# TensorE's expert loop starts on a fetch block boundary and announces its closing branch

## The reference

```python
logits = (t @ w_router + b_router).astype(jnp.float32)
top_val, top_idx = lax.top_k(logits, TOP_K)          # 4 of 32
gate_w = jax.nn.softmax(top_val, axis=-1)
...
def expert_block(args):
    tok_idx, e = args
    xb = t_pad[tok_idx]
    hb = xb @ w_exp_in[e] + b_exp_in[e]               # 1024 -> 2 x 1024
    g = jnp.minimum(hb[:, :D_FF_2], SWIGLU_LIMIT)
    u = jnp.clip(hb[:, D_FF_2:], -SWIGLU_LIMIT, SWIGLU_LIMIT)
    a = g * jax.nn.sigmoid(SWIGLU_ALPHA * g) * (u + 1.0)
    return a @ w_exp_out[e] + b_exp_out[e]            # 1024 -> 1024
```

## Time and profile before

| | us |
|---|---|
| median of 3 runs | 1547.8 (1546.68 to 1548.04) |
| the profiled execution, whole | 1548.02 |
| its span, first to last instruction | 1545.4 |
| TensorE matmuls busy | 1358.8 (88%) |
| VectorE busy | 425.2 (28%) |
| ScalarE busy | 331.7 (21%) |
| GpSimd busy | 121.4 (8%) |
| HBM read | 492.76 MB, 320 GB/s over the span |

### The profile page before, as it was taken

One profiled execution on the slowest core, in us unless ns is written; L12 is line 12 of the kernel. 1 busy time (PEld: TensorE's weight loads), 2 busy tenths in 40 slices (PEclk: granted clock), 3 DMA queues, 4 the chain that ended last, 5 costly groups with the idle time before them and its releaser, 6 DMA issues.

```text
span 1545.4 us, 25866 instructions
## 1 busy us (share of the span) xinstructions
PE 1358.8 (88%) x9234; PEld 788.9 (51%) x9235; DVE 425.2 (28%) x892; ACT 331.7 (21%) x638; POOL 121.4 (8%) x56
## 2 busy tenths in 40 slices
PE   7998999998899998998988788988889988879874
PEld 5554999887789744442343243343323433333421
DVE  0336687753543262111021111111111111111112
ACT  2233566534555211000010010010000101000000
POOL 0000112005665000000000000000000000000000
PEclk9999999999999999999999998999999999999997
DMA  9341366855343198999999999999999999999995
GB/s 334 131 142 55 109 179 188 312 191 183 111 164 134 68 368 326 370 419 418 415 419 418 417 417 418 419 416 420 418 417 417 418 420 415 420 418 417 417 418 241
DMA packets 150051, 494.35 MB, mean 320 GB/s; under 512 B 11665, under 2 KB 59137, under 8 KB 117025
## 3 DMA queue, kind: packets, MB, share of 16 engines
q1 hardware_dynamic: 148531, 491.52, 81.1%
q10 hardware_dynamic: 1486, 2.34, 0.4%
HBM read 492.76 MB, written 1.06 MB: 320 GB/s over the span
## 4 chain that ended last, share of the span: by engine, by line
PE 58%; DMA 19%; SPq 12%; DVE 4%; issue 3%; ACT 3%; ACTq 0%; DVEq 0%
DMA big_mem<-in_w_exp_in 13%; PE ps L863 12%; SPq L404 8%; PE ps L902 6%; DMA big_mem<-in_w_exp_out 6%; PE ps L644 5%; PE ps L645 5%; PE ps L646 5%; PE ps L846 5%; PE ps L477 4%; SPq L401 3%; PE ps L774 2%; PE ps L782 2%; PE ps L616 2%; PE ps L668 1%
## 5 line engine op out<-in xcount | busy, mean ns | idle before, releaser
L863 PE MATMUL ps<-big_mem,ring_mem 128*32 128x512 f32 (+1 forms) x2304 | 391.9, 647 | 63.4 <-DMA big_mem<-in_w_exp_in 63.4
L863 PEld LDWEIGHTS ps<-big_mem,ring_mem 128*32 128x32 f32 (+1 forms) x2304 | 107.5, 124 | 321.3 <-issue 197.0
L902 PE MATMUL ps<-big_mem,x 128*32 128x256 f32 (+1 forms) x1888 | 183.3, 430 | 12.8 <-DMA big_mem<-in_w_exp_out 8.1
L644 PE MATMUL ps<-hT_hi,w_hi 128*128 128x256 f32 x600 | 172.0, 287 | 1.1 <-DVE hT_lo L1422 1.1
L645 PE MATMUL ps<-hT_lo,w_hi 128*128 128x256 f32 x600 | 171.1, 285 | 0.0
L646 PE MATMUL ps<-hT_hi,w_lo 128*128 128x256 f32 x600 | 171.0, 285 | 0.0
L846 PEld LDWEIGHTS ps<-ring_mem,h 128*128 128x128 f32 x1056 | 135.6, 202 | 64.6 <-issue 63.5
L846 PE MATMUL ps<-ring_mem,h 128*128 128x96 f32 x1056 | 153.5, 292 | 0.6 <-DVE ring_mem L1775 0.6
L1816 DVE TENSOR_SCALAR ring_mem<-ps 128x256 f32<-128x256 f32 (+1 forms) x36 | 18.7, 520 | 438.8 <-PE ps L863 438.8
L902 PEld LDWEIGHTS ps<-big_mem,x 128*32 128x32 f32 (+1 forms) x1888 | 69.6, 115 | 112.7 <-issue 64.8
L1335 ACT ACTIVATE ring_mem<-ring_mem 128x256 f32<-128x256 f32 (+1 forms) x36 | 17.7, 493 | 497.9 <-DVE ring_mem L1816 497.9
(11 more groups left out here) (284 smaller groups left out, 1328.0 us busy)
## 6 DMA issues: line engine op xcount, KB each, us to landing
big_mem<-in_w_exp_in SPq DMA_DIRECT2D x256, 1024.0 KB, 19.4
big_mem<-in_w_exp_out SPq DMA_DIRECT2D x256, 512.0 KB, 19.0
ring_mem<-in_w_in SPq DMA_DIRECT2D x15, 2048.0 KB, 8.0
ring_mem<-in_w_up SPq DMA_DIRECT2D x44, 512.0 KB, 4.9
ring_mem<-in_w_down SPq DMA_DIRECT2D x5, 2048.0 KB, 8.7
ring_mem<-in_w_out SPq DMA_DIRECT2D x4, 2048.0 KB, 8.7
ring_mem<-in_w_branch_a SPq DMA_DIRECT2D x1, 2048.0 KB, 7.5
ring_mem<-in_w_branch_b SPq DMA_DIRECT2D x1, 2048.0 KB, 7.4
```

Of the source, the lines that this page charges most:

```text
L644: mm(out, hi, x_hi, start=start, stop=False)
L863: last = mm(out, stationary, weights[:, f, w * q:w * (q + 1)] if m > XS else weights[:, :, w * q:w * (q + 1)], start=start, stop=stop)
L902: last = mm(ps[m * q:m * (q + 1), 4 + at // XS, 0:w], aT[:, k % n, k // n, :], wout[:, k, w * q:w * (q + 1)], start=(k == 0), stop=(k == K ...
```

## The change

```diff
@@ -975,7 +975,7 @@
             nth_reg = pe.alloc_register("pe_nth")
             for r in (next_extra, next_more, nth_reg):
                 pe.reg_mov(r, 0)
-            with pe.Fori(0, E) as e:
+            with nc.Fori(0, E, engines=[mybir.EngineType.PE], hint_back_edge=True, head_slot={mybir.EngineType.PE: 0}) as e:
                 landed_all = 16 * e + 16
                 extra = pe.snap(extra_reg, min_val=0, max_val=TRIO - 1)
                 more = pe.snap(more_reg, min_val=0, max_val=PASSES - 1)
```

## The result

The changed kernel takes 1552.39 us in the median of 7 runs (1550.15 to 1553.93); the kernel before, run beside it, takes 1547.68 us (7 runs, 1546.55 to 1549.52). The ratio is 1.003, 95% interval [1.0018, 1.0041]. The change makes the kernel slower, by 4.7 us or 0.3%, and the interval leaves out 1; forecast were 5.3 us, a time of 1553.1.

What follows compares the result with a forecast made beforehand. TensorE until about 621 us, then the weight transfers, were taken to bound the kernel. Entry wait 3.5, clock 1.7 and second announcement 0.1 made 5.3 us, added to 1547.8 for 1553.1 us, range 1547.5 to 1557.2.

Steps and rivals of the forecast that it cites:

- What bounds the kernel: TensorE's delays between 577 and about 621 us pass one for one to the end; after that weight transfers bound.
- The second hole: Near-idle weight transfers at 618 to 622 us, ending when TensorE frees a buffer in its second pass.
- What the 4.44 us are: Issue time ahead of TensorE's second pass: L995's jump at 611.0 us waits 6.04 us for code not fetched.
- B: Rival, chance 0.06: announcement changes fetch order, L995's wait falls to 0.21 us; gain at most 4.1 us, 1543.7.
- (1) The announcement: Announcing the loop's closing branch saves nothing and adds one instruction a pass, 0.1 us, between 0 and 0.2.
- (2), (3) Padding and place: Branch over padding, 0.2 us, and L990's first jump waiting for the second piece: 3.5 us together, at most 5.8.
- (4) The clock: Idle ahead of the first pass brings one more half-clock stretch on TensorE: 1.7 us, bounds 0 and 3.4.
- The sum: 3.5 + 1.7 + 0.1 = 5.3 us, all ahead of the transfers' idle stretch at 618 to 622 us.
- The signs: Profile after: L990 about 3.9 us, SyncE's issues at about 591 and 626 us, L995 about 6, L978 208 ns.
- (5) L995's wait stays: The 6.04 us wait at 611.0 us, a jump from third to sixth piece, remains; another branch is announced.
- A: Rival, chance 0.20: no wait at the loop's entry, the second piece being there in time; 1548.1 us.
- C: Rival, chance 0.03: announced target refetched every pass, back edge waits, 180 us more on TensorE; 1657 us.

Runs made afterwards that it cites:

- the pause ahead of the loop: Three register loads from memory put ahead of the loop in the kernel before, some 2.0 us together; 1551.24 us, 1.0026.
- slot-0 run: Only the loop's head placed at slot 0, no announcement, against the kernel before; 1552.35 us, 1.0036.
- slot 200: The changed kernel, announcement included, with the loop's head at slot 200 instead of 0; 1553.88 us, 1.0048 of the kernel before.
- slot-40 run: Head at slot 40, closing branch not announced, L995's jump announced at the 64-row form's start, against the kernel before; 1550.20 us, 1.0022.
- the last run with slot 0: Head at slot 0 and L995's jump announced in the first round only, against the kernel before; 1546.91 us, 0.9996.

## Why the prediction was right, point by point

- **What bounds the kernel**: held. The second hole moved as a whole with the first L863 group, 4.7 us of TensorE became 4.7 us of time, and the pause ahead of the loop cost without any fetch. What didn't hold is "after that nothing does": where the two-block rounds begin, waits of 4.47 and 6.13 us cost 3.7 and 4.7 us of transfers (400 and 395 GB/s from 740 to 830 us), and 1.3 us in every round cost 6.9 in all.
- **What the 4.44 us are**: shown. Announcing that jump takes it from 6.04 to 0.34 us and the second hole with it. Where nothing is lost near 750 us it is worth 1547.32 - 1541.75 = 5.6, 1547.42 - 1543.23 = 4.2 and 1547.42 - 1542.92 = 4.5 us in three kernels. B's size for it, the 4.1 us in which the transfers stood idle, was about right; as the most that could be gained it is not refuted by the 5.6, whose interval is 2.9 to 6.8 us.
- **(1) The announcement**: 31 ns, 55 at most, taken at 100. It saves nothing, as said, and alone it changes nothing measurable (1.0004). That the closing branches themselves rose from 208 to 226 ns wasn't foreseen and is hidden.
- **(2), (3) Padding and place**: the step was right in kind and 0.7 us too large. Padding branch 0.32 and L990's 2.86 less its 0.37 make 2.8 us, against 3.5. The term that was mis-sized is the time from entering the head's piece to the start of the fetch. I took 1.45 us, which is counted from the start of L990's jump, and added it behind the end of the branch into the head's piece. That branch ends at 581.5 us and a piece is moved from about 582.3 us, some 0.8 us later.
- **(4) The clock**: 1.6 us against 1.7, by one stretch of 3.4 us at 0.50. The slot-0 run (15.82 for 14.43), slot 200 (15.77) and the pause (16.10) have it too. In the slot-40 run and the last run with slot 0 it was the forecast's upper bound of two stretches, 2.75 and 2.86 us. TensorE had 3.55 and 3.57 us without a matmul there, against 2.30 to 3.47 in the four others; no run shows that this is the reason. That one stretch came here, as I took it, is in part luck.
- **The gather**: not in the sum. 6.77 for 6.34 us in this one execution; 6.50 with the place alone, 6.77 again with slot 200, and 6.28 to 6.53 in the other profiles. It may be scatter between executions; no run settles it.
- **The sum**: 5.3 forecast, 4.7 measured. It comes this near partly because the gather's 0.4 us, which was not in it, stands against the 0.7 us that the wait was taken too long.
- **The signs**: SyncE's first issue came at 589.3 us (591 forecast) and the second at 624.5 (626), both earlier than forecast, as the wait was shorter.
- **(5) L995's wait stays**: 6040 ns.
- **The rivals**: A fell with L990's 2858 ns; its reason, a head near a boundary, was true in part, the head stood between slots 40 and 64. C fell with 226 ns. B is not what the change does, but what announcing the other branch does.

## What to carry to other kernels

Code that a loop runs for the first time is fetched one piece of 256 instructions ahead; a first jump over more than that waits 3 us with idle transfers and 6 with full ones, and a back edge over code already seen waits for nothing. This was measured for TensorE in this kernel alone. So look in the sequencer's rows for the branch whose longest time is thirty times its median, announce that one, from inside its own piece, and leave alone a closing branch that never waits. Moving a loop's head onto a boundary takes away what the code ahead of it had fetched; it costs only if the first pass is on the path, which is also the only place where saving it pays.

## What the runs showed of the hardware

- An announcement executed before its branch's piece is entered replaces the fetch of the next piece in sequence (the 4.47 and 6.13 us waits near 750 us); executed inside that piece it brings the target in addition. The Trainium skill, Runtime: NRT & Kernel Launch, Instruction fetch mechanics, calls the fetching ahead purely sequential; the jumps of 339 to 449 ns, 6038 without the announcement, show a target fetched ahead.
- Two pieces asked for at once under full transfers delay the jump to 7.3 and 7.6 us, from 6.0.
- The wait for a piece under idle transfers was 2.9 to 3.6 us by the branch (2858, 2963, 2997, 3248, 3579 ns), at full ones 5.95 to 6.2 us.
- 2.30 us without a matmul were enough for the granted clock to fall to 0.50 for 3.4 us, which cost 1.7 us. After 3.55 and 3.57 us it was at 0.50 for some 6.8 us, part of it still idle, and cost 2.75 and 2.86 us; after 3.47 us it cost 1.3.
